# A hybrid decoder step in split fp32: another order at the ends of the feed-forward runs, a place of its own for one output tile, and moved sums

## The reference

```python
def swiglu_ffn(h, w_in, w_out):          # D_MODEL 1024, D_FF 2816
    g, u = jnp.split(h @ w_in, [D_FF], axis=-1)
    return (jax.nn.silu(g) * u) @ w_out

...
        yp = yp + op
        ys = ys + os_
        yp = yp + swiglu_ffn(rmsnorm(yp, norm_ffn[i]), w_ffn_in[i], w_ffn_out[i])
        ys = ys + swiglu_ffn(rmsnorm(ys, norm_ffn[i]), w_ffn_in[i], w_ffn_out[i])
    y_prompt = rmsnorm(yp, norm_final)
    y_sample = rmsnorm(ys, norm_final)
```

## Time and profile before

| | |
|---|---|
| median of 3 runs | 1299.27 us (1298.8 to 1299.37) |
| profiled execution, its own time | 1299.66 us |
| its span, first to last instruction | 1297.8 us |
| mean granted clock of PE | 0.99 |
| PE busy | 1265.7 us, 98% |
| DVE, ACT, POOL busy | 839.9, 533.2, 488.2 us |
| matmuls | 9444 |

### The profile page before, as it was taken

How to read it: one execution, slowest core, us unless ns; L and a number is a source line. 1 busy time by engine, 2 the same in 40 slices (tenths; PEclk the granted TensorE clock), 3 DMA queues, 4 the chain that set the end, 5 groups by cost and what they waited for, 6 DMA issues and landing times.

```text
span 1297.8 us, 23232 instructions
## 1 busy us (share of the span) xinstructions
PE 1265.7 (98%) x9444; PEld 1220.3 (94%) x9444; DVE 839.9 (65%) x1359; ACT 533.2 (41%) x950; POOL 488.2 (38%) x252
## 2 busy tenths in 40 slices
PE   9999999899999999999999999899999999999997
PEld 8888899899999999998899999799999999999996
DVE  4776757981288417858547788578981388428754
ACT  5565545452255314542023344224452255315531
POOL 1000043334344433446665544364434334334440
PEclk9999999999999999999999999899999999999998
DMA  8511122222222322233232333123222222323322
GB/s 311 175 34 50 50 66 82 65 98 85 79 98 86 101 88 72 97 114 105 76 114 70 131 118 120 51 67 119 70 89 97 69 95 98 98 66 98 100 80 74
DMA packets 37610, 121.83 MB, mean 94 GB/s; under 512 B 5649, under 2 KB 9681, under 8 KB 36065
## 3 DMA queue, kind: packets, MB, share of 16 engines
q1 hardware_dynamic: 33680, 107.01, 25.3%
q10 hardware_dynamic: 3824, 13.34, 2.8%
HBM read 112.86 MB, written 9.44 MB: 94 GB/s over the span
## 4 chain that ended last, share of the span: by engine, by line
PE 89%; issue 4%; DVE 3%; POOL 2%; ACT 1%; DMA 0%; POOLq 0%; ACTq 0%; SPq 0%; DVEq 0%
PE ps L662 28%; PE ps L664 27%; PE ps L663 27%; POOL wlo L612 1%; PE ps L791 1%; PE ps L838 1%; PE ps L814 1%; PE ps L1120 1%; ACT whi L2085 1%; PE ps L1127 1%; DVE S L1831 1%; DVE acc L1254 1%; DVE ring_sum L1513 0%; PE ps L1111 0%; PE ps L1147 0%
## 5 line engine op out<-in xcount | busy, mean ns | idle before, releaser
L612 POOL TENSOR_TENSOR wlo<-wst,whi 128x1024 fp32r<-128x1024 f32 x101 | 252.2, 2497 | 353.3 <-ACT whi L2085 350.5
L662 PE MATMUL ps<-hid,whi 128*128 128x288 f32 x704 | 209.8, 298 | 3.8 <-POOL wlo L612 2.9
L662 PE MATMUL ps<-xhi,whi 128*128 128x288 f32 x688 | 209.0, 304 | 1.1 <-DVE wlo L1330 0.7
L663 PE MATMUL ps<-hid,whi 128*128 128x288 f32 x704 | 209.0, 297 | 0.0
L664 PE MATMUL ps<-hid,wlo 128*128 128x288 f32 x704 | 208.9, 297 | 0.0
L663 PE MATMUL ps<-xlo,whi 128*128 128x288 f32 x688 | 202.9, 295 | 0.0
L664 PE MATMUL ps<-xhi,wlo 128*128 128x288 f32 x688 | 202.2, 294 | 0.0
L621 POOL TENSOR_TENSOR wlo<-wst,whi 128x512 fp32r<-128x512 f32 x72 | 105.1, 1463 | 202.8 <-ACT whi L2147 202.8
L2085 ACT ACTIVATE whi<-wst 128x1024 fp32r<-128x1024 f32 x66 | 69.9, 1059 | 170.7 <-PE ps L664 170.7
L662 PEld LDWEIGHTS ps<-hid,whi 128*128 128x128 f32 x704 | 133.1, 189 | 5.7 <-POOL wlo L612 4.3
L662 PEld LDWEIGHTS ps<-xhi,whi 128*128 128x128 f32 x688 | 129.0, 187 | 9.6 <-issue 8.3
(11 more groups left out here) (279 smaller groups left out, 3067.8 us busy)
## 6 DMA issues: line engine op xcount, KB each, us to landing
wst<-w_blocks_in SPq DMA_DIRECT2D x188, 512.0 KB, 3.5
S<-s_in ACTq DMA_DIRECT2D x4, 1024.0 KB, 4.9
s_sample_out<-S ACTq DMA_DIRECT2D x4, 1024.0 KB, 4.3
bias<-bias_in SPq DMA_DIRECT2D x1, 2048.0 KB, 11.2
y_out<-x SPq DMA_DIRECT2D x14, 144.0 KB, 1.9
x<-x_in SPq DMA_DIRECT2D x4, 288.0 KB, 7.0
x<-x_in ACTq DMA_DIRECT2D x4, 288.0 KB, 6.0
ktx<-ktx_in SPq DMA_DIRECT2D x1, 1024.0 KB, 12.7
```

The lines of the kernel that those rows point to most:

```text
L612: nc.gpsimd.tensor_tensor(wlo[:, n % RING, :], wst[:, slot, :], raw(whi[:, n % RING, :]), ALU.subtract).then_inc(w_split, 1)
L662: mm(out, stat[0], mov[0], start=start, stop=False, skip_group_check=skip)
L663: mm(out, stat[0], mov[1], start=False, stop=False, skip_group_check=skip)
```

## The change

- `ring(n)`: the block of the third GLA output tile (B_O1 + 2) has its hi and lo in a place of its own, `o1hi` and `o1lo`, which lies over chunks 6 and 7 of xhi and xlo. POOL may split it as soon as the last input tile (B_O1 - 1) is through.
- Feed-forward, PE: in the last pair of each phase product 2 stands ahead of `left_up` and product 6; the first down tile does 2 chunks instead of 3 ahead of the last `left_up`; the order in which the operands' lo halves are counted (`LOWS`) is new.
- Feed-forward, DVE: at the start of a run the sums S1 and S2 and the low halves stand in another order, with B22, T3 and T4 behind the last direct tile's products.
- Feed-forward, ACT: at the start A11, A12 and S1 stand ahead of `silu(3)`; the hi halves of S4 and S3 of each phase's first pair stand behind the copy of product 1; `hidden_high(3)` stands behind the copy of product 5.
- The sample tokens are spread inside `prepare(2, 7)`, ahead of the last addition of squares.
- The first sums over tokens stand behind the first half of the last tile; one scaling less stands ahead of `last_tile(1)`.

```diff
+        o1hi = at("o1hi", x_at[0] + 6 * N * 4, [P, 1024], FR)
+        o1lo = at("o1lo", x_at[0] + (KC + 6) * N * 4, [P, 1024], FR)
...
+        def ring(n):
+
+            return (o1hi[:, :], o1lo[:, :]) if n == B_O1 + 2 else (whi[:, n % RING, :], wlo[:, n % RING, :])
+
...
-                    pool.wait_ge(*used(n - RING))
+                    pool.wait_ge(*used(B_O1 - 1 if n == B_O1 + 2 else n - RING))
...
                     product(5, "S1", "T1", f, 7, True)
+                    if f == pairs_of(phase_of(f))[-1]:
+                        product(2, "A12", "B21", f, 6, True)
                     if before is not None:
                         left_up(before)
                     pe.wait_ge(copied[1], o)
                     product(6, "S2", "T2", f, a, False)
-                    product(2, "A12", "B21", f, 6, True)
+                    if f != pairs_of(phase_of(f))[-1]:
+                        product(2, "A12", "B21", f, 6, True)
...
-                    down(ph, 0, 0, 3)
+                    down(ph, 0, 0, 2)
                     left_up(fs[-1])
-                    down(ph, 0, 3, f1 - f0)
+                    down(ph, 0, 2, f1 - f0)
...
             def last_down():
 
-                pe.wait_ge(acc_done, KC * 5 - 1)
-                for a in range(2):
-                    token_sums(a, acc, True)
...
                     ins.then_inc(last_half, 1)
+                    if a == 0:
+                        pe.wait_ge(acc_done, KC * 5 - 1)
+                        for half in range(2):
+                            token_sums(half, acc, True)
...
+            def spread_samples():
+
+                dve.wait_ge(lo_done, KC * 3)
+                for dst, src in ((shi, xhi), (slo, xlo)):
...
+                if k == 2 and m == KC - 1:
+                    spread_samples()
                 dve.wait_ge(sq_done, m + (KC * k + 1))
...
                 gate(2)
                 operand_low("B11")
                 operand_low("B21")
-                operand_low("B22")
                 up(2)
                 operand_low("T1")
-                operand_low("T3")
+                sum_s1(N_DIRECT)
                 hidden_low(2)
                 gate(3)
+                sum_s2(N_DIRECT)
                 operand_low("T2")
-                operand_low("T4")
-                sum_s1(N_DIRECT)
-                sum_s2(N_DIRECT)
                 sum_low("S1", N_DIRECT)
-                up(3)
                 sum_s4(N_DIRECT)
                 sum_low("S2", N_DIRECT)
-                hidden_low(3)
+                operand_low("B22")
+                up(3)
                 sum_s3(N_DIRECT)
                 sum_low("S4", N_DIRECT)
+                operand_low("T3")
                 sum_low("S3", N_DIRECT)
+                hidden_low(3)
+                operand_low("T4")
...
-            for m in range(4):
+            for m in range(3):
                 scaled(0, m)
             last_tile(1)
-            for m in range(4, 7):
+            for m in range(3, 7):
...
                 hidden_high(2)
+                for q in ("A11", "A12", "S1"):
+                    quarter_high(q, N_DIRECT)
                 silu(3)
-                for q in ("S1", "S2", "A11", "A12"):
-                    quarter_high(q, N_DIRECT)
-                hidden_high(3)
-                for q in ("S4", "S3"):
-                    quarter_high(q, N_DIRECT)
+                quarter_high("S2", N_DIRECT)
...
                         copy(1, f)
+                        if f == fs[0]:
+                            for q in ("S4", "S3"):
+                                quarter_high(q, f)
...
-                        if f > fs[0]:
+                        if f > fs[0] or f == N_DIRECT:
                             hidden_high(f - 1)
...
                     if ph < 2:
-                        for q in ("S1", "S2", "A11", "A12", "S4", "S3"):
+                        for q in ("S1", "S2", "A11", "A12"):
                             quarter_high(q, nxt)
```

More of the change, by code:

```diff
@@ L106 @@
 OPERANDS = ("B11", "B21", "B22", "T1", "T3", "T2", "T4")
+LOWS = ("B11", "B21", "T1", "T2", "B22", "T3", "T4")
 def ordinal(l, f):
@@ L605, in split @@
                     pool.wait_ge(arrived[slot], 16 * (n // STAGE + 1))
-                    pool.wait_ge(*used(n - RING))
-                    nc.gpsimd.tensor_tensor(whi[:, n % RING, :], wst[:, slot, :], zero[:, :].broadcast_to([P, 1024]),
+                    pool.wait_ge(*used(B_O1 - 1 if n == B_O1 + 2 else n - RING))
+                    nc.gpsimd.tensor_tensor(ring(n)[0], wst[:, slot, :], zero[:, :].broadcast_to([P, 1024]),
                                             ALU.add).then_inc(hi_split, 1)
@@ L611, in split @@
                     pool.wait_ge(act_split, NOT_OWN.index(n) + 1)
-                nc.gpsimd.tensor_tensor(wlo[:, n % RING, :], wst[:, slot, :], raw(whi[:, n % RING, :]),
-                                        ALU.subtract).then_inc(w_split, 1)
+                hi, lo = ring(n)
+                nc.gpsimd.tensor_tensor(lo, wst[:, slot, :], raw(hi), ALU.subtract).then_inc(w_split, 1)
             def quarter_low(q, l, f):
@@ L664, in three, with feature_block @@
                 return mm(out, stat[1], mov[0], start=False, stop=stop, skip_group_check=skip)
-            def feature_block(b, slot, src, c0, nch, first, last, fresh=None, part=None):
+            def feature_block(b, n, src, c0, nch, first, last, fresh=None, part=None):
                 lo, hi = part or (0, nch)
+                w_hi, w_lo = ring(n)
                 for c in range(lo, hi):
@@ L674, in feature_block @@
                         s = slice(a * H, (a + 1) * H)
-                        ins = three(ps[:, b + a, 0:H], (whi[:, slot, w], wlo[:, slot, w]),
+                        ins = three(ps[:, b + a, 0:H], (w_hi[:, w], w_lo[:, w]),
                                     (src[0][:, c0 + c, s], src[1][:, c0 + c, s]),
@@ L767, in _ @@
             pe.wait_ge(*split_of(B_K))
-            feature_block(6, B_K % RING, xs, 0, KC, True, True, part=(0, 4))
+            feature_block(6, B_K, xs, 0, KC, True, True, part=(0, 4))
             norm_sums(0, 0, True)
-            feature_block(6, B_K % RING, xs, 0, KC, True, True, part=(4, KC)).then_inc(w_used, 1)
+            feature_block(6, B_K, xs, 0, KC, True, True, part=(4, KC)).then_inc(w_used, 1)
             pe.wait_ge(std_done, 1)
@@ L1239, in gain @@
                 return gains[:, k, m:m + 1] if isinstance(m, int) else gains[:, k, bass.ds(m, 1)]
+            def spread_samples():
+                dve.wait_ge(lo_done, KC * 3)
+                for dst, src in ((shi, xhi), (slo, xlo)):
+                    ins = nc.vector.tensor_copy(
+                        dst[:, :, :].rearrange("p k (j r i) -> p k j r i", j=4, r=2)[:, :, :, 0, :],
+                        src[:, :, NP_TOK:N].rearrange("p k (j i) -> p k j i", j=4))
+                ins.then_inc(samples_spread, 1)
             def prepare(k, m, first=False):
@@ L1675, in _ @@
                                   ).then_inc(sums_spread, 1)
-            for dst, src in ((shi, xhi), (slo, xlo)):
-                ins = nc.vector.tensor_copy(
-                    dst[:, :, :].rearrange("p k (j r i) -> p k j r i", j=4, r=2)[:, :, :, 0, :],
-                    src[:, :, NP_TOK:N].rearrange("p k (j i) -> p k j i", j=4))
-            ins.then_inc(samples_spread, 1)
             nc.vector.memset(AT[:, :, :], 0.0)
```

22 lines of the change are left out of this document (10 added, 12 removed).

## The result

The changed kernel takes 1284.48 us (median of 4 runs, 1282.61 to 1285.57), the kernel before, run beside it, 1299.03 us (1298.46 to 1299.37). The ratio is 0.9889, 95% interval 0.9876 to 0.9902: 14.5 us faster, against 13.8 forecast. The profiled execution of the changed kernel is the shortest of the four: 1282.61 us, with a span of 1280.8.

What follows compares the result with a forecast made beforehand. TensorE was taken as the bound, busy 1265.7 of 1297.8 us, so every term is a stall or clock effect. Terms sum to 13.8 us, giving 1285.5 us against a median of 1299.27; own range 1282.5 to 1288.5, overall 1279.0 to 1289.5.

Steps and rivals of the forecast that it cites:

- Third gated output tile: PE's 4.20 + 0.16 us wait at 834.07 for POOL's split goes, and the slow clock behind it: +6.6 us.
- Phase starts: At starts of phases 1 and 2, PE no longer waits for ACT's copy of product 1: 4 x 0.84, +3.4 us.
- First down tile, end of each phase 2: One more chunk behind left_up covers the last hidden tile's lateness: 2 x 0.62, +1.25 us.
- First down tile, start, all six phases: The first down block's split starts later, behind ACT's copy of product 6: a loss, 6 x 0.35, -2.1 us.
- Rival 2: At the first down tile only the ring slot counts, six stalls vanish: 5.9 us more, 1279.6; chance 0.07.
- Sample spread: PE's 1.15 + 0.16 us wait for slo at 608.32 shrinks to 0.35: +0.95, or +1.3 if copies aren't held up.
- Last sums: At the last tile, the 2.57 + 0.16 us wait for squares goes, a 0.65 wait for wlo comes: +3.6 us.
- Start of the seven products: Both layers' stalls before product 1 move to product 5 of the second pair: +1.8 before clock effects, +0.1 net.
- I take one of two: Start of the seven products: one of the two moved stalls is followed by a slow clock stretch, costing 1.5 us.
- Rival 1: The start is free, DVE isn't late at the first gates: 8.1 us more, 1277.4; chance 0.12.
- rival 3: The third output tile's split waits behind another in POOL, the stall at 834 stays: 6.6 less, 1292.1; chance 0.04.
- rival 4: Slower than before: the later start leaves DVE behind all run, 30 pairs losing 0.5 each give 1300.5; chance 0.03.

Runs made afterwards that it cites:

- The experiment: Changed kernel with the first token sums ahead of the last tile again and four chunks scaled ahead of its row: 1289.34 us, ratio 0.9924 to the kernel before.
- the gates first: Low halves, sum_s4 moved behind first gates or up_right, against changed kernel plus B22 low earlier, first down block split early, last block's low earlier: 1274.51 us, ratio 0.981.
- Filling idle time: Changed kernel with VectorE making the low half of B22 ahead of sum_s4 at the start of both layers: 1282.51 us in its one run.

## Why the prediction was right

**Third gated output tile** (+6.6, measured +6.5). Both terms hold. The tile waits for the first to be added to x, at the place forecast: DVE ends at 825.22, PE starts at 825.27. Putting it back costs 5.8 by medians.

**Phase starts** (+3.4, measured +3.8) and **First down tile, end of each phase 2** (+1.25, measured +1.4): right; the longer step behind each stall was left out. Undoing the former alone brought back its four waits in full. The latter was not undone by itself; the trace shows its two waits gone and no other in their place.

**First down tile, start, all six phases** (-2.1, measured -1.7). The edit that looks like a gain is a loss, for the reason given; the size is 0.30 instead of 0.35. Rival 2 (only the ring slot counts) falls.

**Sample spread** (+0.95, measured +1.0). What was left open was whether a copy of one input is held up by POOL. It is, in full:

```profile
600.77 2.50 DVE L1257 CAST shi<-xhi 128x512 fp32r<-128x512 f32 x1
603.19 0.41 DVE L1257 CAST slo<-xlo 128x512 fp32r<-128x512 f32 x1
...
600.19 2.79 POOL L620 TENSOR_TENSOR wlo<-wst,whi 128x1024 fp32r<-128x1024 f32 x1
```

The first copy takes 2.50 us instead of 0.41 and ends 0.29 behind POOL's operation; the second, behind it, is free. The step left at 603.65 is 0.27 longer than an undisturbed one (0.35 forecast). The Trainium skill (GPSIMD Engine Reference, Specifications) speaks of contention with instructions in a 2-port mode or with two SBUF inputs, and by this rule the copy can be held up only if it runs in a 2-port mode. The row agrees with that, and none shows the mode itself.

**Last sums** (+3.6, measured +3.6). The wait for wlo is 0.71 (0.65 forecast). The experiment adds that this term holds a slow stretch, which cost 1.5 us more in another execution.

**Start of the seven products** (+0.1, measured +0.6 in the profiled execution). The chain was right: product 5 of the second pair was forecast 14.8 us behind the last direct tile, and starts 14.77 behind it in layer 0 and 14.76 in layer 1 (before, 16.32 and 15.11). Its terms hold too: from the tile's end DVE works through its list with no gap above 0.13, and POOL takes the forecast 2.2 of it. The step that failed is the one from there to the gain. The +1.8 before clock effects lacked `left_up`'s wait for up_right, 0.42 in each layer, which stood only in the range, and what the first matmuls behind each of these stalls take longer, some 0.25 in each layer. From product 5 to the end of product 7 it is 10.1 us instead of 9.4, and +0.6 is left. "I take one of two" slow stretches at 1.5 us: the table gives 7 in 18, at 1.0. With one of them the term is -0.4. So the +0.1 came near by two errors that cancel: 1.3 us of cost left out, and 1.5 us taken for a slow stretch that the profiled execution doesn't have. Rival 1 (the start is free) falls; so does rival 3, as POOL does the third tile's split at 805.16; and so does rival 4, since all pairs from the third on run without a wait, in the profiled execution and in all the others.

**The sum.** 1285.5 against 1284.48. The profiled execution was forecast at 1285.9 and took 1282.61; of these 3.3 us the clock at both ends of the program is 1.85, and the start, the first down tiles, the phase starts and ends the rest. The places and mechanisms are as forecast; that the medians agree within 1.0 us is in part luck, since the median also holds slow stretches whose number was guessed.

**What the forecast missed** was not in the change but next to it: the first down tile's 0.77 went away altogether by another order, for which POOL had 7 us of room. I had priced the edit and not asked which other order the same rows allow.

## What to carry to other kernels

When work is moved so that a stall goes, count the queue behind the new place: the busy time that stands ahead of the next consumer says when that one starts (14.8 forecast, 14.77 measured). Another order in a late queue only chooses which consumer waits: with the gates first, product 5 started 1.9 us earlier and product 7 at the same time as before. Filling idle time (1.06 us) made the whole earlier. A wait on a copy can be a matter of one instruction standing ahead of it in its queue; look there first, and for idle time on the engine that makes the late operand. A stall of some 2 us or more can cost more than its length, by a slow stretch that follows in some executions and not in others.

## What the runs showed of the hardware

- An idle time of 2.24 to 2.52 us on PE was followed by the 1.2 GHz clock in 7 of 18 cases and by full clock in 11, within one kernel too; one of 1.85 in 1 of 2, one of 2.02 in 2 of 2. Once it was there, the 36 matmuls behind took 1.0 us more (0.9 to 1.0, once 2.2).
- DVE's copy from SBUF with one input is held up by POOL as one with two is: 2.50 us instead of 0.41 (128 x 512), beside POOL's 2.79. The effect ends with POOL's instruction; DVE's next is at its usual length.
- The first 18 us of the span took 1 us longer in the trace before than in the one after, with the same matmuls in the same order. Before, the matmuls of 256 columns are 0.21 apart until 13.3 us, after 0.12 from the second on. That this is a clock that rises later is an inference from the spacing; the profile's granted clock is 1.00 in both. In two of the experiments the spacing is 0.21 up to 10.7 and 11.4 us, and they are no later at 16 us than the others, as PE then waits less for its operands. The two timelines of PE:

```profile
7.93 0.41 PE L664 MATMUL ps<-whi,xlo 128*128 128x256 f32 x1
8.15 0.41 PE L662 MATMUL ps<-whi,xhi 128*128 128x256 f32 x1
```
```profile
7.96 0.28 PE L670 MATMUL ps<-wlo,xhi 128*128 128x256 f32 x1
8.08 0.28 PE L671 MATMUL ps<-whi,xlo 128*128 128x256 f32 x1
```
